# Experts of a routed layer in plain fp32, two at a time in the halves of TensorE's columns, with a ring of nine 1 MB slabs

## The reference, cut to what matters

```python
def grouped_moe(x, router_w, router_bias, w_gate_up, w_down):
    t = x.reshape(-1, D)                                   # 256 tokens, D = 1024
    scores = jax.nn.sigmoid((t @ router_w))                # 16 experts
    biased = scores + router_bias
    grp = biased.reshape(T, N_GROUPS, EXPERTS_PER_GROUP)   # 4 groups of 4
    sel_group = jnp.argmax(jnp.sum(lax.top_k(grp, 2)[0], -1), -1)
    ...                                                    # the 2 best experts inside that group
    gates = ...                                            # normalised unbiased scores of the two
    h = jnp.einsum('td,edf->tef', t, w_gate_up)            # 1024 -> 2 x 256 for each expert
    a = jax.nn.silu(h[..., :256]) * h[..., 256:] * gates[..., None]
    return jnp.einsum('tef,efd->td', a, w_down)            # 256 -> 1024
```

## Time and profile before

| | before |
|---|---|
| median of 3 runs (lowest, highest) | 1739.92 us (1739.51, 1740.38) |
| span of the profiled execution | 1735.7 us |
| PE busy | 1645.2 us, 95% |
| DVE, ACT busy | 1051.7 us, 894.7 us |
| bytes moved, mean rate | 327.61 MB, 189 GB/s |
| granted PE clock, mean | 0.971 of 2.4 GHz |

### The profile page before, as it was taken

How to read it: one execution, slowest core, us unless ns; L and a number is a source line. 1 busy time by engine, 2 the same in 40 slices (tenths; PEclk the granted TensorE clock), 3 DMA queues, 4 the chain that set the end, 5 groups by cost and what they waited for, 6 DMA issues and landing times.

```text
span 1735.7 us, 24248 instructions
## 1 busy us (share of the span) xinstructions
PE 1645.2 (95%) x7774; PEld 1355.9 (78%) x7774; DVE 1051.7 (61%) x1323; ACT 894.7 (52%) x1325; POOL 88.1 (5%) x154
## 2 busy tenths in 40 slices
PE   7998999799899997999999999998999999999997
PEld 6877788687678886888788778887888788778885
DVE  4565889747559886555556654455554457655544
ACT  5653677457347774444455554444444455554443
POOL 1410000014000000000020000000000020000000
PEclk9996999899879998999999999999999999999999
DMA  7522699562239995655563555654556552555561
GB/s 230 194 74 99 243 352 351 173 208 100 67 115 366 346 346 168 193 183 187 169 194 122 171 170 192 190 178 159 177 192 193 185 185 97 193 165 188 181 193 61
DMA packets 197275, 327.61 MB, mean 189 GB/s; under 512 B 12378, under 2 KB 109376, under 8 KB 196672
## 3 DMA queue, kind: packets, MB, share of 16 engines
q1 hardware_dynamic: 196432, 323.66, 56.1%
q0 software_dynamic: 752, 2.82, 0.6%
HBM read 325.38 MB, written 1.05 MB: 188 GB/s over the span
## 4 chain that ended last, share of the span: by engine, by line
issue 61%; PE 31%; DVE 3%; ACT 2%; DVEq 1%; POOL 1%; DMA 1%; POOLq 1%; SPq 0%; ACTq 0%
PE bank L368 8%; PE bank L370 8%; PE bank L369 8%; PE bank L721 1%; PE bank L954 1%; PE bank L825 1%; ACT sb_arena L1260 1%; DVEq L1742 0%; PE bank L993 0%; DVE sb_x L1752 0%; ACT sb_whi L359 0%; DVE sb_wlo L364 0%; PE bank L972 0%; PE bank L994 0%; DMA sb_raw<-w_in 0%
## 5 line engine op out<-in xcount | busy, mean ns | idle before, releaser
L364 DVE TENSOR_TENSOR sb_wlo<-sb_raw,sb_whi 128x1024 fp32r<-128x1024 f32 x614 | 713.7, 1205 | 436.7 <-ACT sb_whi L359 435.9
L359 ACT ACTIVATE sb_whi<-sb_raw 128x1024 fp32r<-128x1024 f32 x616 | 606.3, 1036 | 388.5 <-PE bank L370 386.1
L368 PE MATMUL bank<-sb_whi,sb_op_hi 128*128 128x512 f32 (+3 forms) x1280 | 500.2, 391 | 15.4 <-DVE sb_op_lo L1896 8.5
L370 PE MATMUL bank<-sb_whi,sb_op_lo 128*128 128x512 f32 (+3 forms) x1280 | 492.7, 385 | 0.0
L369 PE MATMUL bank<-sb_wlo,sb_op_hi 128*128 128x512 f32 (+3 forms) x1280 | 492.6, 385 | 0.0
L368 PEld LDWEIGHTS bank<-sb_whi,sb_op_hi 128*128 128x128 f32 x1280 | 246.3, 192 | 64.0 <-DVE sb_op_lo L1896 10.1
L370 PEld LDWEIGHTS bank<-sb_whi,sb_op_lo 128*128 128x128 f32 x1280 | 246.1, 192 | 47.7
L369 PEld LDWEIGHTS bank<-sb_wlo,sb_op_hi 128*128 128x128 f32 x1280 | 246.6, 193 | 44.6
L368 PE MATMUL bank<-sb_whi,sb_lat_hi 128*128 128x512 f32 (+2 forms) x552 | 213.0, 386 | 9.1 <-DVE sb_lat_lo L1572 6.0
L370 PE MATMUL bank<-sb_whi,sb_lat_lo 128*128 128x512 f32 (+2 forms) x552 | 212.2, 384 | 0.0
L369 PE MATMUL bank<-sb_wlo,sb_lat_hi 128*128 128x512 f32 (+2 forms) x552 | 211.8, 384 | 0.0
(11 more groups left out here) (223 smaller groups left out, 1182.5 us busy)
## 6 DMA issues: line engine op xcount, KB each, us to landing
sb_raw<-ffn_w SPq DMA_DIRECT2D x264, 512.0 KB, 4.3
sb_raw<-exp_w_gate_up SPq DMA_DIRECT2D x128, 512.0 KB, 5.2
sb_raw<-w_in SPq DMA_DIRECT2D x84, 512.0 KB, 4.6
sb_raw<-exp_w_down SPq DMA_DIRECT2D x64, 512.0 KB, 5.1
sb_raw<-w_out SPq DMA_DIRECT2D x32, 512.0 KB, 4.4
sb_raw<-w_branch_pool SPq DMA_DIRECT2D x8, 512.0 KB, 4.1
sb_raw<-w_branch_attn SPq DMA_DIRECT2D x8, 512.0 KB, 5.2
sb_raw<-w_in SPq DMA_DIRECT2D x8, 288.0 KB, 5.0
```

Of the source, the lines that this page charges most:

```text
L359: nc.scalar.activation(h, r, ACT.Copy).then_inc(hi_made.sem, 1)
L364: nc.vector.tensor_tensor(o, r, h.bitcast(F32), ALU.subtract).then_inc(lo_made.sem, 1)
L368: nc.tensor.matmul(ps, hi, wh, start=first, stop=False)
L370: return nc.tensor.matmul(ps, lo, wh, start=False, stop=last)
```

## The change

- Experts are computed with plain fp32 products, straight from the loaded slab: no split of expert weights or of the gathered tokens, and 1 product in place of 3.
- An expert has 64 slots of its own (`CAP`) in place of a group's 128. Experts run in pairs: one's result goes to PSUM partitions 0 to 63, the other's to 64 to 127, so one uses the left half of the array's columns and the other the right half. The branch is now on `size > CAP`: an expert with more than 64 tokens sends the layer through a way that multiplies all 256 tokens by every expert in fp32.
- During the experts the nine buffers of the ring (`raw`, `whi`, `wlo`) are nine slots of one ring of 1 MB slabs, each loaded by one transfer with 8 KB in a row for each partition. The first nine slabs are requested as the last slabs of `w_out` leave their buffers.
- The router slab is gone. `router_w` is loaded once at the start, and the router is a plain fp32 product with the logits' rows in the four column quarters (`router`), summed by a product with a 0/1 matrix (`fold`). DVE ranks experts and groups by comparisons (`ranks`), both for experts and for groups before the count.
- Gathering for experts 8 to 15, the turned slot matrices and the slot gates (`late_gather`, `pair_slots`) move in between the pairs. The code of the eight pairs is written out, without a loop.
- The `w_ukv` slab of the mixer is now two slabs of half the width, so a layer still has a multiple of three slabs (18).

```diff
+MOE_RING = 3 * RING
+PAIRS = NE // 2
+CAP = P // 2
+MOE = 6 * PAIRS
...
+                for i in range(RING):
+                    number = slab_number(0, S1, l, S1 - RING + i)
+                    expert_slab(raw_slot + i, lambda: sp.wait_ge(lo_made.sem, number * 2 + (2 + 2 * RING)))
+                for i in range(RING):
+                    number = slab_number(0, S1, l, S1 - RING + i)
+                    expert_slab(whi_slot + i, lambda: sp.wait_ge(slab_done.sem, number + (1 + RING)))
+                    expert_slab(wlo_slot + i, lambda: None)
...
+                for s in range(MOE_RING, MOE):
+                    expert_slab(s, lambda: moe_done(sp, l, s - MOE_RING))
...
+                def router(ch):
                     for k in range(DK):
...
+                        r = slice(32 * (k % 4), 32 * (k % 4) + 32)
+                        i = nc.tensor.matmul(bank[4 + 2 * ch][r, 0:P], rw[:, NE * k:NE * k + 32], xT[:, k, ch * P:ch * P + P], start=k < 4, stop=k >= 4)
...
+                def pair_up(p):
+                    if p:
+                        wait(F, "aT_out", l, p)
+                    if p == 4:
+                        wait(F, "xg_d", l, 12)
+                    for h in range(2):
+                        w = expert_slabs(up_slab(p, h))
+                        for k in range(4):
...
+                            for e, r in enumerate(streams):
+                                o = CAP * ((2 * p + e) % 8)
+                                i = nc.tensor.matmul(bank[4][r, :], xg[:, p // 4, 4 * h + k, o:o + CAP], w[e][:, 512 * k:512 * k + 512],
+                                                     start=h == 0 and k == 0, stop=h == 1 and k == 3)
...
+                def pair_down(p):
+                    w = expert_slabs(down_slab(p))
+                    if p:
+                        wait(F, "y_lo", l, 2 * p)
+                    else:
+                        wait(F, "xg_d", l, 6)
+                    wait(F, "aT_out", l, p + 1)
+                    for nh in range(2):
+                        for f in range(2):
+                            for e, r in enumerate(streams):
+                                o = D * f + 512 * nh
+                                i = nc.tensor.matmul(bank[6 + nh][r, :], pair_aT[:, p % 2, f, CAP * e:CAP * e + CAP], w[e][:, o:o + 512], start=f == 0, stop=f == 1)
...
+                    for p in range(PAIRS):
+                        pair_up(p)
+                        pair_slots(p)
+                        if p:
+                            pair_down(p - 1)
+                        if p < 4:
+                            late_gather(2 * p)
+                        pair_turn(p)
+                        if p >= 2:
+                            scatter(p - 2)
+                        if p < 4:
+                            late_gather(2 * p + 1)
+                    pair_down(PAIRS - 1)
+                    scatter(PAIRS - 2)
+                    scatter(PAIRS - 1)
...
+                    for p in range(PAIRS):
+                        products_done(p)
+                        nc.scalar.activation(pair_sg, bank[4][:, 0:FE], ACT.Silu).then_inc(F["sg"].sem, 1)
+                        wait(F, "slot", l, p + 1)
...
+                        nc.scalar.activation(of_slot[p], bank[5][:, 0:T], ACT.Copy).then_inc(F["of_slot"].sem, 1)
+                        if p:
+                            down_hi(p - 1)
+                    following(0)
+                    down_hi(PAIRS - 1)
```

More of the change, by code:

```diff
@@ L1631, in _ @@
                     i.then_inc(F["lat_lo"].sem, 1)
-                for j in range(6, 12):
+                for j in range(6, 13):
                     lo1(l, j)
@@ new lines, in _ @@
+                four = lambda name, groups: c(name).unsqueeze(1).to_broadcast([P, groups, 4])
+                step(tt(biased, scores, rbias[:].unsqueeze(1).to_broadcast([P, NC, 16]), ALU.add))
+                grouped = biased.rearrange("p c (g n) -> p (c g) n", g=4)
+                ranks(grouped, 8, above, beats, order)
+                step(tt(sel, order, four("two4", 8), ALU.is_lt))
+                step(tt(best, grouped, sel, ALU.mult))
+                step(nc.vector.tensor_reduce(gscore, best, axis=AX.X, op=ALU.add))
@@ L1886, in _ @@
+                layer_norm(2, lambda ch, nh: wait(F, "y", l, (1, 3)[nh] if ch == 0 else 4), "x_ready")
             with dve.Fori(0, DEPTH) as l:
```

696 lines of the change are left out of this document (377 added, 319 removed).

## The result

The changed kernel takes 1670.9 us (median of 4 runs, 1667.04 to 1674.83) against 1740.15 (1739.51 to 1741.17) for the kernel before, a ratio of 0.960 with a 95% interval of 0.959 to 0.962: 4% faster. The forecast was 1670 with a range of 1648 to 1700. The agreement is closer than the working deserves, and is luck to that extent: the routed layers gained 15 us more than forecast, and a loss that the forecast did not contain, in products outside the experts, took 17 us. The profiled execution has a span of 1667.8 us, and 67.9 us less than 1735.7 is what has to be explained.

The account below looks back on a forecast made before the run. PE was taken to set the pace, with transfers following closely. A layer gains 148.4 - 122 + 6.5 + 1.8 = 34.7 us, two layers 69.4, so 1739.92 - 69.4 = 1670 us, range 1648 to 1700.

Parts of the forecast that it names:

- Products of a pair: Experts' stretch: both column halves run at once, so a pair's up products take 6.9 us, its down products 3.5.
- Rival (a): Experts' products: the two column halves take turns, a pair costs 10.4 us more, the time is 1828 us; chance 4%.
- The rest on PE: Experts' stretch: with slots, late gathers, scatters, turns, switches and first-pair waits, PE needs 118 us for 148.4.
- Transfers: Expert slabs: at 375 GB/s the ring costs 4 us more than PE alone, making the stretch 122 us.
- rival (c): Expert slabs: transfers bind at 330 to 349 GB/s, stretch 129 to 135 us, time 1684 to 1696; chance 14%.
- Routing: Layer norm to first up product: it comes 6.5 us earlier a layer, between 0 and 9 depending on the clock.
- End: Last down product to the statistics: 2.9 us instead of 4.7, a gain of 1.8 us a layer.
- Edges: Outside the routed layers: the split w_ukv slab shifts the mixer's later slabs in the ring; 0, within 1 us.
- Rival (e): Everything better: 400 GB/s, the clock rises in the residuals, switches cost nothing; 1651 us, chance 8%.
- (b): Experts' stretch: the clock stays at 1.2 GHz, 83 us become 166, the time is 1828 us; chance 3%.
- (d): Experts' pairs: hand-overs among PE, ACT and DVE leave 2 us a pair uncovered, 1702 us; chance 5%.
- (f): Experts' branch: one expert with over 64 tokens takes the other way, 338 us for 122, time 2100; chance 1%.

Follow-up runs that it names:

- e3: The changed kernel with a pair's up products in alternating blocks of eight rows and down products in blocks of four, not row by row: 1704.7 us.
- e5: The changed kernel with all 16 up rows of one expert of a pair ahead of all 16 of the other, down products still interleaved: 1757.2 us.
- e6: The changed kernel with the second residual moved back behind the count, where the kernel before had it: 1674.4 us.
- e1: The changed kernel with 128 unused bytes a partition ahead of op_hi and op_lo, which then start 128 past a multiple of 512: 1652.4 us.
- e9: The changed kernel with 64 unused bytes a partition ahead of op_hi and op_lo, which then start 64 past a multiple of 512: 1657.6 us.

## Why the prediction was right, and where it was not

Time and direction came out as forecast, but as a sum of misses that cancel. Term by term:

**Products of a pair**: right. The two halves run at once with 512 columns too, 32 up rows and their switch take 7.01 us, forecast 7.05. Rival (a), that the halves take turns, falls on the same row. The price of taking turns was also overdrawn: even with the experts' blocks one after another, e3 came to 1705 and e5 to 1757, not 1828, since rows of the two halves pass each other.

**The rest on PE**: the sum of 118 us was right, 117.3 and 115.6 measured; of these 2.9 are idle in the first layer, where the forecast had 2 for it. The two layers differ by the first up products, which in the first run partly on the slow clock (8.78 us above; this is the second layer's row):

```profile
460.56 7.09 PE L1070 MATMUL bank<-sb_moe,sb_xg 128*64 128x512 f32 x32 [2.50 <-issue]
```

**Transfers**: the step that was sized wrongly within the routed layers. 375 GB/s was taken as what the engines give, and made the ring set 122 us. They give 424, and PE sets 117. The argument that stood against rival (c) (PE asked for no more) was right and should have been used on the forecast itself: a rate measured while another engine sets the pace is a lower bound. The trace of before even had 397 over 10 us, which the working passed over. The stretch is 4.7 and 6.4 us shorter than forecast; 4 of this in each layer is the ring, the rest PE's own sum. The forecast also has a slip here: 17.5 + 98 is 115.5, and the last landing was put at 117.5 with no reason given for the 2 us. Rival (c) falls.

**Routing**: 8.6 and 8.1 us gained between x and the first up product, with 5.6 in the sum. The choice came at x + 10.1 us, as forecast. But in the first layer the clock rose while the residuals ran (8 rows in 5.07 us, where 7.1 was forecast), so PE reached the count when DVE did and not 2 us later. In the second it rose later:

```profile
440.58 6.23 PE L788 MATMUL bank<-sb_x,sb_const 128*128 128x512 f32 x8
446.64 0.29 PE L1021 MATMUL bank<-sb_small,sb_const 128*128 128x16 f32 x2
```

The count then starts at x + 10.9 us, and eight of the gathers behind it run on the slow clock. The prediction had a rise with the residuals as the other end of its bound, 9 us, and took the low clock for this term. Between the two traces, e6 puts the residuals' place at 2.0 and 1.8 of the 3.0 and 2.5 us that came beyond the 5.6. (The 7.1 us are twice the first residual of before, 157.90 to 161.45 in the earlier trace rows; the 163.45 to 166.22 that the prediction cites for it are 2.8 us, a misreading that changed nothing.) The 0.9 us for an earlier layer norm did not come: from the statistics to x there are 8.87 us in both kernels.

**End**: 2.0 for 1.8 us. Right.

**Edges**: the step that failed. "Same bytes, other halves: 0, within 1 us either way" holds for the slabs' order: with op back in place (e1) the three stretches are 1.1 us longer than before. But 16.9 us were lost there, 15.8 of them by the move of two tiles, which the prediction had at nothing. The size fits the pace: between the changed kernel and e1 a row differs by 5.0 ns, and the 3480 distances of full-width rows on op would make 17.4 us of it, for the 15.8 measured. The profile of before could have warned: its up products, whose stationary tile does not start as the slabs do, took 233 ns a row beside down products at 226 to 227. The move was in the diff, and it had no row, no bound and no sentence. With this loss the sum would have been 1670 + 17 = 1687 and the routed layers' surplus of 15 us would have been the miss. The forecast of 1670 was met because the two cancel, which is luck. Rival (e), "everything better", named 1651. Without the loss (e1) the kernel reached 1652, with two of (e)'s three causes in part: transfers above 400 GB/s and a clock that rises in the routing; the switches were not free, but cost what was forecast.

**Rivals (b), (d) and (f)**: the clock is at 0.99 in the experts' stretch; PE waits for DVE in the first pair, at one late gather and ahead of the fifth pair alone, less than 3 us in all in the first layer; the branch was not taken, as the 32 rows on 64 columns show.

## What to carry over

Read the whole diff for moves of tiles, not only for work. Before a tile that PE streams or loads is moved, note where it lies within 256 bytes against its partner, and afterwards compare distances of starts in stretches that the change should not touch; a uniform 2% there is worth as much as a stage. Work in two column halves should alternate between them row by row, or in blocks of up to four rows; blocks of eight already lose, and what lies between was not run. A transfer rate read while PE sets the pace is a lower bound, and a ring can live above the engines' rate for as long as what it fetched ahead lasts.

## What the runs showed of the hardware that was not expected

- A stream of fp32r products of 512 columns takes 227 ns a row when the stationary tile and the streamed one start alike within 256 bytes, and 232.5 when they differ by 128 (eight kernels; 1.0% of the time of a program that is mostly such products). With the stationary tile 64 short of the streamed one it takes 229 (e9), with it 64 past 233 (up products of before).
- PE starts rows of one column half ahead of earlier rows of the other: blocks of four rows cost 3.70 us for 3.65, blocks of eight 8.97 for 7.09, blocks of sixteen 12.29.
- One core moves 424 GB/s from HBM with 8 KB in a row and 1 MB a request, 386 to 406 with 2 and 4 KB.
- A load of one value into a PE register and the branch on it left gaps of 2.95 and 2.50 us between products in the two layers; with the load moved some 7 us ahead 1.70 and 1.76 remained.
